# Hybrid decoder block: both compressions' products move between the two halves of a projection block

## The reference

```python
mod = (jax.nn.silu(c) @ w_ada[l] + b_ada[l])[:, None, :]
sh1, sc1, gt1, sh2, sc2, gt2 = jnp.split(mod, N_MOD, axis=-1)      # 6 x 1024
h = rms_norm(x, g_pre_mix[l]) * (1.0 + sc1) + sh1
proj = h @ w_in[l]
q, kc, vc, ksl, vsl, kwn, vwn, nsa_g, u, br_g = jnp.split(proj, IN_SPLITS, axis=-1)
kc_c = compress(rope(kv(kc)), cmp_pe_k[l], cmp_w1_k[l], cmp_w2_k[l])
vc_c = compress(kv(vc), cmp_pe_v[l], cmp_w1_v[l], cmp_w2_v[l])

def compress(k, pe, w1, w2):          # 63 overlapping blocks of 32 tokens, one every 16
    blk = k[:, idx] + pe[None, None, :, None, :]
    blk = blk.transpose(0, 1, 3, 2, 4).reshape(b, n_cmp, g, CMP_BLOCK * dh)
    return jax.nn.gelu(blk @ w1) @ w2
```

## Time and profile before

| | |
|---|---|
| median of the runs | 1478.3 us (1478.2 to 1479.91) |
| the profiled execution | 1479.48 us |
| its span | 1477.7 us, 1.8 us less than its time |
| TensorE matmul busy | 1414.5 us, 96% |
| VectorE busy | 1070.7 us, 72% |
| ScalarE busy | 646.5 us, 44% |
| GpSimd busy | 328.6 us, 22% |
| DMA | 208.31 MB, mean 141 GB/s |
| mean granted TensorE clock | 0.991 |

### The profile page before, as it was taken

How to read it: one execution, slowest core, us unless ns; L and a number is a source line. 1 busy time by engine, 2 the same in 40 slices (tenths; PEclk the granted TensorE clock), 3 DMA queues, 4 the chain that set the end, 5 groups by cost and what they waited for, 6 DMA issues and landing times.

```text
span 1477.7 us, 19532 instructions
## 1 busy us (share of the span) xinstructions
PE 1414.5 (96%) x7206; PEld 1182.6 (80%) x7206; DVE 1070.7 (72%) x1479; ACT 646.5 (44%) x1124; POOL 328.6 (22%) x429
## 2 busy tenths in 40 slices
PE   3898999999999999989999999999999999999997
PEld 3786778888888888768887877888888888888885
DVE  5759844677877878885432788877777797777778
ACT  4534524555665666663122664222222434343342
POOL 2314432333322322111210410000000030404034
PEclk9999999999999999999999999999999999999999
DMA  9377856322221211016453424544443773535226
GB/s 354 89 244 256 266 121 169 86 75 60 64 62 47 57 56 34 19 63 194 142 182 103 143 75 156 197 157 156 147 145 136 270 286 113 199 109 204 87 84 228
DMA packets 131750, 208.31 MB, mean 141 GB/s; under 512 B 19525, under 2 KB 84549, under 8 KB 128071
## 3 DMA queue, kind: packets, MB, share of 16 engines
q1 hardware_dynamic: 128074, 196.61, 40.6%
q0 software_dynamic: 3584, 10.49, 2.1%
HBM read 146.24 MB, written 54.53 MB: 136 GB/s over the span
## 4 chain that ended last, share of the span: by engine, by line
PE 80%; DVE 10%; ACT 3%; issue 3%; SPq 2%; DMA 2%; POOL 0%; DVEq 0%; POOLq 0%; ACTq 0%
PE ps L2071 17%; PE ps L2072 17%; PE ps L2073 17%; PE ps L2077 5%; PE ps L2078 5%; PE ps L2079 5%; PE ps L2271 4%; PE ps L2287 2%; PE ps L2288 2%; PE ps L2238 2%; PE ps L2239 2%; DVE acc L1559 1%; DMA ada<-in_w_ada 1%; SPq L539 1%; DVE ada_acc L1434 1%
## 5 line engine op out<-in xcount | busy, mean ns | idle before, releaser
L2071 PE MATMUL ps<-act_hi,a_hi 128*128 128x512 f32 x448 | 190.8, 426 | 0.5 <-DVE a_lo L1413 0.5
L2073 PE MATMUL ps<-act_hi,a_lo 128*128 128x512 f32 x448 | 175.6, 392 | 0.0
L2072 PE MATMUL ps<-act_lo,a_hi 128*128 128x512 f32 x448 | 175.2, 391 | 0.0
L2071 PE MATMUL ps<-wr_hi,left_hi 128*128 128x512 f32 x320 | 124.5, 389 | 0.0
L2072 PE MATMUL ps<-wr_lo,left_hi 128*128 128x512 f32 x320 | 124.5, 389 | 0.0
L2073 PE MATMUL ps<-wr_hi,left_lo 128*128 128x512 f32 x320 | 124.5, 389 | 0.0
L1615 DVE TENSOR_TENSOR pt_lo<-ps,pt_hi 128x512 fp32r<-128x512 f32 (+1 forms) x160 | 103.1, 644 | 19.8 <-ACT pt_hi L1152 18.3
L1334 ACT ACTIVATE left_hi<-left_st 128x2048 fp32r<-128x2048 f32 x28 | 53.6, 1915 | 144.1 <-PE ps L2073 81.8
L1254 ACT ACTIVATE w_hi<-w1s 128x1024 fp32r<-128x1024 f32 x54 | 57.0, 1057 | 112.3 <-PE ps L2073 74.8
L1152 ACT ACTIVATE pt_hi<-ps 128x512 fp32r<-128x512 f32 (+1 forms) x160 | 89.0, 563 | 32.6 <-PE ps L2271 30.9
L1739 DVE TENSOR_TENSOR w_lo<-w1s,w_hi 128x1024 fp32r<-128x1024 f32 x54 | 65.9, 1222 | 51.1 <-ACT w_hi L1254 51.0
(11 more groups left out here) (282 smaller groups left out, 3882.7 us busy)
## 6 DMA issues: line engine op xcount, KB each, us to landing
left_st<-h_dram SPq DMA_DIRECT2D x28, 1024.0 KB, 5.1
ada<-in_w_ada SPq DMA_DIRECT2D x48, 512.0 KB, 5.9
h_dram<-hid SPq DMA_DIRECT2D x48, 512.0 KB, 3.1
w1s<-in_w_fc SPq DMA_DIRECT2D x32, 512.0 KB, 4.4
w2s<-in_w_fc SPq DMA_DIRECT2D x16, 1024.0 KB, 7.4
raw<-in_w_in SPq DMA_DIRECT2D x28, 512.0 KB, 4.5
g_dram<-g_out POOLq DMA_DIRECT2D x32, 256.0 KB, 2.4
mg<-g_dram SPq DMA_DIRECT2D x16, 512.0 KB, 3.8
```

The source lines that it names most:

```text
L2071: pe.matmul(dst, wh, mh, start=start, stop=False)
L2072: pe.matmul(dst, wh, ml, start=False, stop=False)
L2073: return pe.matmul(dst, wl, mh, start=False, stop=stop)
```

## The change

In TensorE's program the call `compress(0)` stood behind block 4 and `compress(1)` behind block 6. Now `compress(0)` stands inside block 5 and `compress(1)` inside block 7, each between the block's first and second half, ahead of the second half's waits. No other engine's program is touched.

```diff
             for ch in range(2):
                 g = 2 * a + ch
+                if a == 5 and ch == 1:
+                    compress(0)
+                if a == 7 and ch == 1:
+                    compress(1)
                 if g >= 4:
                     pe.wait_ge(fm_act, g - 3)
                     if a - 2 in FM_ROPE:
                         pe.wait_ge(rope_cos, 2 * FM_ROPE[a - 2] + ch + 1)
                 ins = project(a, g % 4, ch, range(KT))
                 ins.then_inc(fm_mm, 1)
-            if a == 4:
-                compress(0)
-            if a == 6:
-                compress(1)
             if a == 7:
                 second_modulation()
```

## The result

The changed kernel is slower. Over 20 runs each, taken side by side, its median is 1483.6 us (1478.3 to 1486.69) against 1479.05 us before (1476.13 to 1481.02): ratio 1.0028, 95% interval 1.002 to 1.0037, that is 4.1 us with an interval of 3.0 to 5.5 us. The forecast was 1480.0 us and no measurable difference; the value lies beyond the range, and the rival with TensorE's clock low throughout, +4.1 us, is what happened.

The account below looks back on a forecast made before the run. VectorE's chain to the `acc2` additions, not TensorE, was taken to bound the second modulation's start. Compression gap 0 plus clock +1.7 us on the 1478.3 us median gave 1480.0 us; range 1477.1 to 1482.8 us.

Parts of the forecast that it names:

- the rival with TensorE's clock low throughout: Second modulation runs wholly at 1.2 GHz: +4.1 us, 1482.4 us, slower; chance 0.22.
- The hole moves and does not close: TensorE's 6.8 us idle before the first compression moves to 176 us, before the second modulation; gain zero.
- The 1.5 us of idling before the first compression: After half 5,0 ends at 137.70 us, TensorE waits for `bk` until 139.2 us; 1.5 of 6.8 us idle remain.
- The end of the additions holds the modulation, and no link of that chain runs through TensorE: VectorE's additions into `acc2` still end at 182.88 us; between 132 and 182 us nothing there waits for a projection product.
- The compressions themselves cost nothing more: Same matmuls issued at both compressions; the first takes 3.6 us at kept clock; gap at the compressions 0.
- The clock: The moved hole drops TensorE to 1.2 GHz before the second modulation, which then costs +1.7 us; chance 0.45.
- Between them: back after the first four rows ... That is +1.7 us, and I take it: Second modulation: first four rows at 1.2 GHz, then full clock returns, then the same 4.73 and 3.50 us as before.
- The upper bound: Whole second modulation at half clock: 14.14 us against 10.04 us, +4.1 us.
- The argument against the low clock: Only line 2179 ran from 189.47 to 192.97 us, at 0.50, and right behind it the clock was back.
- the forecast's lower end of -1.2 us: Second modulation regains full clock after its first four rows and keeps it: 8.88 us against 10.04 us.

Follow-up runs that it names:

- The filled hole: Changed kernel plus 24 matmuls of 512 columns, read by nobody, between block 7 and the second modulation: median 1477.68 us, ratio 0.9995 to the kernel before.
- the one-column filler: Changed kernel plus 24 fp32 matmuls of one column, read by nobody, between block 7 and the second modulation: median 1483.14 us, ratio 1.0034 to the kernel before.

## Why the prediction was wrong

- *The hole moves and does not close*: right. It went from 6.81 us before the first compression to 5.43 us before the modulation (5.10 and 6.55 us in the other two traces; forecast 6 to 7), with 0.85 us before block 7 (forecast 1.3) and 1.75 us before the second compression (forecast 1.1).
- *The 1.5 us of idling before the first compression*: wrong, without effect on the time. It appeared in none of the three traces, and the kernel before already spoke against it. The prediction let half 5,0 start at 132.26 us, but `a_lo` of block 5 is being written until about 133.4 us:

```profile
131.47 2.01 DVE L1413 TENSOR_TENSOR a_lo<-raw,a_hi 128x1024 fp32r<-128x1024 f32 x1
```

  With it the half ends at 138.9 us and leaves 0.3 us. In the third trace TensorE does wait for it, at the start of block 5:

```profile
134.81 0.50 PE L2071 MATMUL ps<-act_hi,a_hi 128*128 128x512 f32 x1 [1.10 <-DVE a_lo L1413]
```

  In the first two TensorE was later still: it had waited 3.2 and 3.1 us near 121 us, ahead of the change, and part of block 4 then ran at 1.2 GHz (clock 0.55 from 124 to 126 us in the first).
- *The end of the additions holds the modulation, and no link of that chain runs through TensorE*: right. The chain's length was 49.39 us against 49.48 us. The filled hole gave back the loss, which it could not have done for a delay on that chain. The start of the modulation, forecast at 182.9 us within 0.5 us, was missed in all three traces (184.49, 183.95 and 184.84 us), because the chain began later.
- *The compressions themselves cost nothing more*: right, 3.67 and 3.64 us at full clock. The 1.7 us that the first one saved were off the path, as was its hole.
- *The clock*: the mechanism was right, its size was not. **The step that failed is "Between them: back after the first four rows ... That is +1.7 us, and I take it".** I let the clock return after 3.5 us because a compression had got it back after 3.6 us. Measured: the first four rows of line 2179 didn't bring it back in any of the three traces, the one-column rows behind them ran at 0.50 throughout, and the modulation cost +3.88 us. The upper bound, 3.50 + 7.14 + 3.50 = 14.14 us, was nearly exact (13.92 us). I had weighted it 0.22, though the earlier trace rows already showed that those one-column rows lose the clock even when they begin with it; work that had lost the clock was no ground for expecting it back.
- *The argument against the low clock*: a misreading. It said that right behind the last four rows of line 2179 the clock was back, from a mean of 0.99 over 62 us. That mean leaves room for 1 us at 0.50, and the same trace has it:

```profile
193.00:194.00 1.00, 1.00 (x4) 0.81 (x4) 0.89 (x3) 0.00 (x0) 0.00 (x0) 0.50 0.00 0
194.00:195.00 1.00, 1.00 (x6) 0.83 (x5) 0.59 (x3) 0.31 (x1) 0.00 (x0) 1.00 0.02 8
```

  The clock returned at 194.0 us, 1.0 us into block 8. So the kernel before had already shown four rows of line 2179 that ran 3.50 us at 1.2 GHz without raising the clock.
- *The rule of the Trainium skill*: that dense work keeps the clock and a long wait loses it ("TensorE: Matmul & The Clock Gate", section "Loop structure matters more than you think") agrees with the traces here: every hole of 5 us and more in this stage took the clock to 0.50, and 5.60 us of wide matmuls in its place kept it at 1.00. Reading Part 1's "busy" as a full row, which spoke for the forecast's lower end of -1.2 us, is refuted by the one-column filler: row full, clock 0.50.
- *The range*: it ended at 1482.8 us, with 0.4 us for the spread of the runs. The changed kernel's runs spread over 8.4 us, and the kernel before has a median of 1479.05 us over 20 runs where the forecast had 1478.3 us from three. The rival's own price was right, but its side of the range was cut too close for that.

## What to carry to other kernels

When a wait is taken off an engine that doesn't set the end, the idle time goes to the next wait on the true chain; ask what work stands behind it there, and at which clock it will start. For TensorE look at the granted clock and at the shape of the matmuls, not at the busy share: here the one-column matmuls did not keep the clock when they filled a hole, and ran at half of it from end to end behind one. The hole should be given wide work that is needed anyway, and thin matmuls mixed into wide ones; here both together turned a loss of 4.1 us into a gain of 7.7 us.

## What was not expected of the hardware

- 24 fp32 matmuls of one column kept TensorE's row full for 5.84 us and the clock still fell to 1.2 GHz; 24 of 512 columns, 5.60 us, held 2.4 GHz.
- The products of line 2179 stream 512 columns against a weight one column wide, and their effect on the clock was not uniform. At the start of the modulation, 3.51 us of them did not raise it (three traces), and neither did 3.50 us of them at its end in the kernel before. At its end, with the modulation in block 8, 188.98 to 192.12 us, the clock was back at about 191.7, before any other matmul ran. What distinguishes these cases stayed open.
- The 32 one-column rows take 3.73 us at 2.4 GHz and 6.99 us at 1.2 GHz, a factor of 1.87 (both from the first row's start to the last one's end).
